# Moving three small VectorE instructions, a product and a result write by one quarter of a step in the differential attention of an encoder layer

## The reference

```python
def block(qblk):                      # 128 queries of one head, two maps m
    s = jnp.einsum('bhmqd,bhmkd->bhmqk', qblk.astype(jnp.float32) * scale, kf)
    pr = jax.nn.softmax(s, axis=-1)
    a = pr[:, :, 0] - lam * pr[:, :, 1]
    return jnp.einsum('bhqk,bhkd->bhqd', a, vf)
...
o = rms_norm(o, subln_g, SUBLN_EPS) * (1.0 - lam_init)
```

## Time and profile before

| | |
|---|---|
| median of three runs | 3232.36 us (3229.59 to 3234.27) |
| the profiled execution | 3234.27 us, span 3232.5 us |
| TensorE matmuls busy | 3123.7 us (97%) |
| VectorE, ScalarE, GpSimd busy | 1811.2, 1553.7, 1369.7 us |
| mean granted TensorE clock | 0.987 of full speed |

### The profile page before, as it was taken

One profiled execution on the slowest core, in us unless ns is written; L12 is line 12 of the kernel. 1 busy time (PEld: TensorE's weight loads), 2 busy tenths in 40 slices (PEclk: granted clock), 3 DMA queues, 4 the chain that ended last, 5 costly groups with the idle time before them and its releaser, 6 DMA issues.

```text
span 3232.5 us, 48938 instructions
## 1 busy us (share of the span) xinstructions
PE 3123.7 (97%) x17504; PEld 2700.2 (84%) x17504; DVE 1811.2 (56%) x3103; ACT 1553.7 (48%) x2824; POOL 1369.7 (42%) x1116
## 2 busy tenths in 40 slices
PE   8999999999999999997999999899989999999998
PEld 8988889788888899996887787677768888888787
DVE  5133432898989956664555665766534554442222
ACT  4011110787888878882235555555543334333332
POOL 2123331011111156662245657666666666665222
PEclk9999999999999999998999999999989999999999
DMA  5233335303041347755754765377586678665221
GB/s 166 99 107 122 121 119 164 85 22 86 22 93 41 80 104 184 181 131 177 246 177 153 251 225 170 127 249 250 188 264 199 200 234 269 197 200 204 74 74 56
DMA packets 467407, 493.43 MB, mean 153 GB/s; under 512 B 84064, under 2 KB 377312, under 8 KB 461920
## 3 DMA queue, kind: packets, MB, share of 16 engines
q1 hardware_dynamic: 463824, 484.02, 49.0%
q10 hardware_dynamic: 3344, 6.29, 0.8%
HBM read 322.05 MB, written 168.17 MB: 152 GB/s over the span
## 4 chain that ended last, share of the span: by engine, by line
PE 74%; DMA 8%; POOL 6%; ACT 5%; issue 3%; DVE 2%; SPq 1%; POOLq 0%; ACTq 0%; DVEq 0%
PE c_pv L844 6%; PE h_acc L136 6%; PE h_acc L137 6%; PE h_acc L138 6%; PE a_acc L138 5%; PE a_acc L137 5%; PE a_acc L136 5%; DMA e_a<-w_up_dram 4%; PE b_pv L984 4%; PE c_scores L825 3%; PE c_scores L826 3%; PE c_turned L833 3%; PE b_scores L1236 3%; PE b_turned L1246 2%; ACT e_a_hi L1784 2%
## 5 line engine op out<-in xcount | busy, mean ns | idle before, releaser
L2297 POOL TENSOR_TENSOR h_u_lo<-h_u_raw,h_u_hi 128x512 fp32r<-128x512 f32 x224 | 375.8, 1702 | 208.1 <-ACT h_u_hi L2293 208.1
L136 PE MATMUL h_acc<-h_w_hi,h_u_hi 128*128 128x512 f32 x896 | 350.9, 392 | 13.2 <-POOL h_u_lo L2297 7.1
L137 PE MATMUL h_acc<-h_w_lo,h_u_hi 128*128 128x512 f32 x896 | 350.2, 391 | 0.0
L138 PE MATMUL h_acc<-h_w_hi,h_u_lo 128*128 128x512 f32 x896 | 350.1, 391 | 0.0
L2391 DVE TENSOR_TENSOR h_h<-h_acc,h_h 128x512 f32<-128x512 f32 x224 | 154.2, 689 | 327.7 <-PE h_acc L138 323.2
L741 DVE TENSOR_REDUCE c_neg_half<-c_scores 128x1 f32<-128x1024 f32 x256 | 312.7, 1222 | 43.9 <-PE c_scores L826 43.9
L136 PE MATMUL e_acc<-e_b_hi,e_a_hi 128*128 128x512 f32 x768 | 305.1, 397 | 29.6 <-ACT e_u L2043 19.5
L698 ACT ACTIVATE c_e<-c_scores,c_neg_max 128x1024 f32<-128x1024 f32 x256 | 286.3, 1119 | 67.2 <-DVE c_neg_max L748 67.2
L137 PE MATMUL e_acc<-e_b_lo,e_a_hi 128*128 128x512 f32 x768 | 302.3, 394 | 0.0
L138 PE MATMUL e_acc<-e_b_hi,e_a_lo 128*128 128x512 f32 x768 | 302.2, 393 | 0.0
L844 PE MATMUL c_pv<-c_v,c_at 128*128 128x128 f32 x2048 | 270.3, 275 | 0.4 <-ACT c_o L712 0.4
(11 more groups left out here) (201 smaller groups left out, 7931.7 us busy)
## 6 DMA issues: line engine op xcount, KB each, us to landing
h_u_raw<-s_u SPq DMA_DIRECT2D x224, 256.0 KB, 3.5
s_u<-e_u SPq DMA_DIRECT2D x192, 256.0 KB, 3.1
s_qkt<-a_hl SPq DMA_DIRECT2D x128, 256.0 KB, 2.8
e_a<-w_up_dram SPq DMA_DIRECT2D x64, 512.0 KB, 4.8
h_w_raw<-s_t SPq DMA_DIRECT2D x32, 1024.0 KB, 7.9
h_w_raw<-w_down_dram SPq DMA_DIRECT2D x24, 1024.0 KB, 7.8
b_kt<-s_qkt SPq DMA_DIRECT2D x64, 256.0 KB, 9.5
e_t<-w_down_dram SPq DMA_DIRECT2D x32, 512.0 KB, 6.1
```

Of the source, the lines that this page charges most:

```text
L136: nc.tensor.matmul(out, lhs_hi, rhs_hi, start=first, stop=False, skip_group_check=onto)
L137: nc.tensor.matmul(out, lhs_hi, rhs_lo, start=False, stop=False, skip_group_check=onto)
L138: return nc.tensor.matmul(out, lhs_lo, rhs_hi, start=False, stop=last, skip_group_check=onto)
L2297: self.nc.gpsimd.tensor_tensor(self.u_lo[q][s][:], self.u_raw[q][s][:], self.u_hi[q][s][:].bitcast(F32), ALU.subtract).then_inc(self.S["u_ ...
```

## The change

The order of VectorE's instructions inside a step. `denominators`, `reciprocal` and `coefficient` of step `n+1` move from quarter 1 to quarter 2, `combine(n+1, 0)` from quarter 2 to the end of quarter 3, and `result(n-2)` from the end of quarter 3 to quarter 2, ahead of the three small ones. The instructions themselves, their waits and all other engines' streams are the same.

```diff
                         if q % 2 == 1 and n + 2 < STEPS:
                             whole(n + 2, q // 2)
-                        if q == 1 and 0 <= n + 1 < STEPS:
+                        if q == 2 and n >= 2:
+                            result(n - 2)
+                        if q == 2 and 0 <= n + 1 < STEPS:
                             denominators(n + 1)
                             reciprocal(n + 1)
                             coefficient(n + 1)
-                        if q == 2 and 0 <= n + 1 < STEPS:
+                        if q == 3 and 0 <= n + 1 < STEPS:
                             combine(n + 1, 0)
-                        if q == 3 and n >= 2:
-                            result(n - 2)
```

## The result

| | before | after |
|---|---|---|
| median of the runs | 3230.98 us (3226.80 to 3234.27, 4 runs) | 3267.84 us (3266.91 to 3270.53, 4 runs) |
| profiled execution, span | 3234.27, 3232.5 us | 3271.68, 3269.9 us |
| mean granted TensorE clock | 0.987 | 0.987 |

The ratio is 1.0119, with a 95% interval of 1.0107 to 1.0131: 1.2% slower, 37 us by the medians of the table. The changed kernel was executed 22 times in all (3265.24 to 3272.78 us, median 3270.1 us), and the ratio is the one that these give: 39 us.

A forecast was written before the change was run, and what follows sets the result against it. TensorE was taken to set the pace; 62 steps x 0.66 us = 40.9 us, less 1.5 us, gave +39.4 us, 3273.7 us for the profiled execution and a forecast median of 3271.8 us, range 3262 to 3291 us.

The forecast's parts named there:

- The pace is TensorE's: Edited stage: TensorE, not VectorE, sets the step of 9.05 us, and what it loses stays lost.
- The small ones gain nothing by leaving quarter 1: VectorE, quarter 1: the room is worthless, as maximum(n+2,2) waits for its scores anyway; gain 0.
- Quarter 2 holds result and the small ones: VectorE, quarter 2: they end before the scores for maximum(n+2,3) are ready, hidden by 0.03 us without overlap.
- rival C: VectorE, quarter 2: the block does not fit and costs 0.3 us a step more, 19 us, 3291 us; chance 6%.
- Combine is late by 0.83 us and costs 0.66 us: Transposes' weight load on TensorE: combine delays it 0.83 us, 0.17 us is absorbed, 0.66 us a step is lost.
- No second wait: Scores on TensorE: the exp that frees their bank ends at 1011.9, before they open at 1013.0.
- Count and ends: Of 64 steps two are free: 62 x 0.66 = 40.9 us, less 1.5 us from fewer waits for stores.
- Other stages only shift: Stages outside the edited one keep their length and only shift by some 40 us.
- A: TensorE within a step: holes take up the loss, no change, 3232 us; chance 3%.
- B: VectorE's order: faster, some 3226 us, if combine(n+1,0) ends before 1008.57; chance 2%.
- D: TensorE's clock: idle holes lower it, 100 us if in every step, about 3372 us; chance 3%.

The follow-up runs named there:

- e4: Changed kernel; on TensorE alone values(n-1,0) goes ahead of turn(n,0) in quarter 0 of each step: 3233.62 us, ratio 1.0015.
- e5: Kernel before; on TensorE alone values(n-1,0) goes ahead of turn(n,0) in quarter 0: 3230.56 against 3229.85 us, ratio 1.0003.
- e1: Kernel before with only combine(n+1,0) moved from quarter 2 to the end of quarter 3: 3268.28 against 3230.13 us, ratio 1.0125.
- e3: Changed kernel with combine(n+1,0) ahead of whole(n+2,1) instead of behind it: 3261.12 us, ratio 1.0100.
- e7: Changed kernel with two more copies of result's instruction in quarter 2, writing to spare buffers: 3289.03 us, ratio 1.0186.
- e2: Changed kernel with combine(n+1,0) back in quarter 2, behind result and the three small instructions: 3260.79 us, ratio 1.0096.
- e9: Kernel before with only denominators, reciprocal and coefficient moved from quarter 1 to quarter 2, ahead of combine: 3243.75 against 3229.71 us, ratio 1.0044.
- e6: Changed kernel with one more copy of result's instruction in quarter 2, writing to a spare buffer: 3274.34 us, ratio 1.0141.
- e8: Kernel before with only result(n-2) moved from quarter 3 to quarter 2, ahead of combine: 3230.84 against 3229.71 us, ratio 1.0000.
- f1: Kernel before with SyncE's loads of the next head issued in five portions over steps 4 to 8: 3227.28 against 3229.85 us, ratio 0.9994.

## Why the prediction was right

**The pace is TensorE's.** Right. The step is 9.05 us (9.07 with the edit of e4 and e5) where TensorE is not held up. It grows by TensorE's wait for combine, less some 0.2 us (after, e1, e3, e7), or by the lateness of the exp beyond a slack (e2, e9).

**The small ones gain nothing by leaving quarter 1.** Right: the maximum behind them now idles for 0.83 us instead of 0.19.

**Quarter 2 holds result and the small ones.** Right (rival C falls): e1 costs as much without them as the changed kernel with them. The cover is 0.24 to 0.28 us (e6, e7), wider than the 0.03 to 0.12 us that I read from the rows: I had counted at most one overlap of 0.09 us, and there are three, of 0.09 us at each of result's two borders and of 0.07 us at the start of the maximum in e7. It holds only because combine left the quarter: with combine in it, the small ones cost 14 us (e9), and both together 31 us (e2).

**Combine is late by 0.83 us and costs 0.66 us.** Right: the step grew by 0.65 us. The waits booked at the weight load and the growth of the step belong together in three runs: 0.69 and 0.48 us (e3), 0.89 and 0.65 us (after), 1.12 and 0.89 us (e7). The growth is the wait less 0.21 to 0.24 us. That is about the lead of this load over its matmul, 0.23 us in the kernel before (1008.62 in the earlier trace rows against the 1008.85 of the row below); three runs fit it, and none varies the lead itself. The wait is booked from the end of the load ahead, from which 0.05 us passed before as well (1008.57 to 1008.62), so the load is late by some 0.84 us, 0.83 forecast, and 0.19 us of it are not paid, 0.17 forecast.

```profile
1008.38 0.19 PEld L826 LDWEIGHTS c_scores<-c_kt_lo,c_qs 128*128 128x128 f32 x1
...
1008.85 0.60 PE L833 MATMUL c_turned<-g_ident,c_a_row 128*128 128x128 f32 x4
```

e4 shows that it is the date and not the order: a later demand on TensorE brings 9 parts in 10 back.

**No second wait.** Right for the change; e2 and e9 show where it lies. With maximum(n+2,3) late by 0.33, 0.77 and 1.03 us the step grew by 0, 0.18 and 0.45 us: this path, by whole and exp to the scores, has some 0.58 us of slack, and in the two runs beyond it the rest counts in full.

**Count and ends.** A little small. The first three steps grew by 1.5 us together and the stage's tail by 1.6 us, where I had counted two steps as free and the last two like others. What came back at the head boundaries is 1.7 us (2.26 us of excess at the two disturbances before, 0.5 us after) against 1.5 us. Of the two reasons that I gave for it, the runs bear out the longer step: result waits for stores for 0 to 0.8 us in all in the runs with a step of 9.50 us or more, and for 1.3 to 4.3 us in those with 9.05 to 9.24 us and undivided loads, whether it has moved (e4, e8) or not (before, e5, e9). The size is less sure: the longest landing of a store varies from 17.9 to 20.3 us between the traces of the kernels with undivided loads. The stage, from VectorE's first maximum to its first instruction of the next, grew from 595.8 to 635.7 us, 39.9 us against the +39.4 us of the sum.

**Other stages only shift.** In the two profiled executions they are together 2.5 us shorter (0.9 us ahead of the stage, 1.6 us behind it), which no part of the change explains and which the scatter of the kernel before (3226.80 to 3234.27 us) contains. It is the difference between 39.9 us and the 37.4 us of the spans. How close the forecast of the time came can be said within this scatter only.

**Rivals A, B, D.** A: a loss of 0.65 us a step would have fitted into the holes of the weight loads' row, and it was paid all the same. That row was 90% busy and yet the step had nothing to spare: here the rule of the Trainium skill (Perfetto Trace Analysis, Identifying the Most-Contended Engine) did not tell the room that TensorE had. B: the load that waits for combine came some 0.84 us late, where B wanted it in time. D: the granted clock stayed at 1.00 with an idle time of 0.46 us in every step.

## What to carry to other kernels

In a schedule written out by hand, write down for each result when the engine that sets the pace asks for it. In this kernel moving an instruction was free up to that date and cost nearly in full past it (all but some 0.2 us of the lateness), whatever its engine's share of busy time. A full engine that waits for the bottleneck has room; which of its gaps may be filled is set by what stands behind the gap, so price a group of moves as a group: two moves that cost 0 and 14 us alone cost 31 us together, and nothing once a third has left the quarter.

## What had not been expected of the hardware

How much of a late weight load was paid differed between two places of the step; that it is the load's neighbours that make the difference fits the rows and was not tested by itself. The transposes' load comes behind matmuls of 512 columns and runs 0.23 us ahead of its own matmul; of a wait there, 0.21 to 0.24 us are not paid. The scores' load comes behind matmuls of 128 columns and usually starts 0.08 us before the last load of that group is over (1004.65 + 0.97 = 1005.62 against 1005.54 in the rows below, of the kernel before); a wait of 0.37 us there cost 0.45 us (e2), and a loss of 0.18 us a step was hardly booked as a wait at all (e9). A row of waits is thus neither an upper nor a lower bound of the loss; the distance from step to step gives the loss.

```profile
1004.65 0.97 PEld L844 LDWEIGHTS c_pv<-c_v,c_at 128*128 128x128 f32 x8
...
1005.54 0.19 PEld L825 LDWEIGHTS c_scores<-c_kt_hi,c_qs 128*128 128x128 f32 x1
```

A store of 64 KB took 20.3 us to land when it was issued behind 5 MB of loads from the same queue (SyncE's issue of it alone lasted 15.05 us), and at most 3.7 us when those were issued in portions of 1 MB (f1).
